# The border between two blocks: residual before split, squares behind the parts, softmax sums behind the gated output

## The reference, cut to what matters

```
x  = x + rms_norm(mixer(rms_norm(x, pre_norm_w)), post_norm_w)      # first block
h  = rms_norm(x, norm_g)                                            # second block
qa, kca, vca, ksa, vsa, kwa, vwa, za, ga, qb, kb, vb, zb = split(h @ w_in_2)
o_a = g0 * compressed(qa) + g1 * selected(qa) + g2 * windowed(qa)   # g = sigmoid(ga)
o_b = banded(qb, kb, vb)                                            # with sinks
x  = x + concat(o_a * silu(za), o_b * silu(zb)) @ w_out_2
out = rms_norm(x, final_g)
```

## Time and profile before

| | |
|---|---|
| median of 3 runs (lowest to highest) | 1212.39 us (1212.36 to 1212.54) |
| the profiled execution's own time | 1211.66 us |
| its span in the trace | 1209.8 us |
| PE busy | 1196.0 us, 99% |
| DVE busy | 750.3 us, 62% |
| ACT busy | 608.6 us, 50% |
| POOL busy | 98.7 us, 8% |

### The profile page before, as it was taken

The page is one execution under the profiler, slowest core; times in us unless marked ns, Lnnn a source line. Parts: engine busy times, 40 slices in busy tenths (PEclk is TensorE's granted clock), DMA queues, the critical chain, the costliest instruction groups (busy, mean ns, idle before and its releaser), DMA issues.

```text
span 1209.8 us, 16240 instructions
## 1 busy us (share of the span) xinstructions
PE 1196.0 (99%) x6422; PEld 999.4 (83%) x6422; DVE 750.3 (62%) x1002; ACT 608.6 (50%) x896; POOL 98.7 (8%) x134
## 2 busy tenths in 40 slices
PE   9999999999999999999999999999999999999997
PEld 8888888888878888888888888888777778788886
DVE  5778876765666656555554455576665665676654
ACT  6665655544324555444444444464446547566443
POOL 0000011189200000000000000010000000000000
PEclk9999999999999999999999999999999999999999
DMA  8666664576544545665666686656747555454862
GB/s 286 172 204 177 187 195 141 163 211 193 175 142 122 174 124 145 217 193 176 200 184 195 194 286 200 201 177 200 239 154 239 164 173 186 121 164 144 297 197 95
DMA packets 143259, 224.03 MB, mean 185 GB/s; under 512 B 12176, under 2 KB 63056, under 8 KB 142160
## 3 DMA queue, kind: packets, MB, share of 16 engines
q1 hardware_dynamic: 140800, 212.50, 57.4%
q0 software_dynamic: 2064, 9.45, 2.2%
q10 hardware_dynamic: 320, 1.06, 0.2%
HBM read 218.25 MB, written 4.72 MB: 184 GB/s over the span
## 4 chain that ended last, share of the span: by engine, by line
PE 94%; DVE 3%; ACT 1%; issue 1%; DMA 0%; POOLq 0%; SPq 0%; POOL 0%; ACTq 0%; DVEq 0%
PE acc L2030 64%; PE acc L2009 10%; PE acc L2011 5%; PE aux L1900 4%; PE acc L1960 2%; PE acc L2021 2%; PE aux L2245 1%; PE aux L2273 1%; DVE lo_w L1357 1%; PE aux L1983 1%; PE aux L2135 1%; PE aux L2238 1%; PE aux L2266 1%; ACT hi_w L981 0%; DVE cv L1476 0%
## 5 line engine op out<-in xcount | busy, mean ns | idle before, releaser
L1357 DVE TENSOR_TENSOR lo_w<-raw_w,hi_w 128x1024 fp32r<-128x1024 f32 (+1 forms) x381 | 464.6, 1226 | 340.0 <-ACT hi_w L981 338.6
L981 ACT ACTIVATE hi_w<-raw_w 128x1024 fp32r<-128x1024 f32 (+1 forms) x381 | 395.3, 1053 | 268.7 <-PE acc L2030 188.5
L2030 PE MATMUL acc<-hi_w,h_both 128*128 128x512 f32 (+1 forms) x1632 | 521.6, 392 | 0.3 <-DVE h_both L1721 0.3
L2030 PEld LDWEIGHTS acc<-hi_w,h_both 128*128 128x128 f32 x1632 | 304.6, 188 | 66.9 <-issue 4.9
L2030 PE MATMUL acc<-lo_w,h_both 128*128 128x512 f32 (+1 forms) x816 | 315.0, 386 | 0.0
L2009 PE MATMUL acc<-h_both,hi_w 128*128 128x512 f32 x576 | 204.1, 399 | 0.5 <-DVE lo_w L1357 0.5
L2030 PEld LDWEIGHTS acc<-lo_w,h_both 128*128 128x128 f32 x816 | 153.5, 188 | 28.1
L2011 PE MATMUL acc<-h_both,lo_w 128*128 128x256 f32 x576 | 160.9, 279 | 0.0
L2009 PEld LDWEIGHTS acc<-h_both,hi_w 128*128 128x128 f32 x576 | 108.2, 188 | 26.3 <-DVE lo_w L1357 0.9
L2011 PEld LDWEIGHTS acc<-h_both,lo_w 128*128 128x128 f32 x576 | 108.6, 189 | 0.1
L2030 PE MATMUL acc<-hi_w,m_hi 128*128 128x512 f32 x224 | 87.7, 391 | 0.0
(11 more groups left out here) (361 smaller groups left out, 1196.9 us busy)
## 6 DMA issues: line engine op xcount, KB each, us to landing
raw_w<-in_w_in SPq DMA_DIRECT2D x279, 512.0 KB, 3.9
raw_w<-in_w_out SPq DMA_DIRECT2D x64, 512.0 KB, 4.6
raw_w<-in_w_branch_a SPq DMA_DIRECT2D x16, 512.0 KB, 4.7
raw_w<-in_w_branch_b SPq DMA_DIRECT2D x16, 512.0 KB, 4.8
raw_w<-in_cmp_k_w SPq DMA_DIRECT2D x8, 512.0 KB, 6.3
raw_w<-in_cmp_v_w SPq DMA_DIRECT2D x8, 512.0 KB, 7.1
x_in<-in_x SPq DMA_DIRECT2D x8, 256.0 KB, 7.3
x<-in_x POOLq DMA_DIRECT2D x1, 2048.0 KB, 10.8
```

The lines of the kernel that those rows point to most:

```text
L981: act.activation(piece_flat(hi_w[slot], no), piece_flat(raw_w[no % RAW_SLOTS], no), ACT.Copy).then_inc(*hi_ready.event(no))
L1357: dve.tensor_tensor(piece_flat(lo_w[slot], no), piece_flat(raw_w[no % RAW_SLOTS], no), piece_flat(hi_w[slot], no).bitcast(F32), ALU.subtra ...
L2030: i = pe.matmul(to[:, t, 0:group.cols], x[at], w[:, k], start=first and k == 0 and m == 0, stop=last and k == n - 1 and m == 2)
```

## The change

Three groups of edits, all in the order of steps. Nothing is computed otherwise.

- Tick c: on DVE and ACT the tick's split of piece c+4 stands behind `h2_hi(1, 0)`, `h2_lo(1, 0)` and `residual(0, 1)`, no longer ahead of `y_last(1)`.
- Ticks c+3 to c+9: `residual(3, t)` goes from c+3 to c+4, behind the parts of quarter 2; the splits of pieces c+7 and c+8 are placed by hand, the latter behind the parts of quarter 3; the eight squares go from c+3, c+5 and c+6 to c+6 and c+7, all behind the parts of quarter 3; `norm2` and `rope_tables` come a tick later.
- Compressed attention: DVE's sums, clamp, inverse and gate go from tick 347 to tick 348, that is behind both `flip("y", 2, t)` and the split of piece 350. The key by which a tick's steps are sorted also names `catt(2)`.

```diff
-    if tick >= TICKS or tick not in FULL or tick == FINAL - 2 or -3 <= tick - BORDER <= 4:
+    if tick >= TICKS or tick not in FULL or tick == FINAL - 2 or -3 <= tick - BORDER <= 6:
...
         for n in ahead:
-            at(c + tick, "split", c + n)
             if n == 4:
                 at(c, "y_last", 1)
+                at(c, "h2_hi", 1, 0)
+                at(c, "h2_lo", 1, 0)
+                at(c, "residual", 0, 1)
+            at(c + tick, "split", c + n)
...
-    at(c, "h2_hi", 1, 0)
-    at(c, "h2_lo", 1, 0)
-    at(c, "residual", 0, 1)
...
     for t in range(NT):
-        at(c + 3, "residual", 3, t)
         at(c + 3, "h2_flip", 2, t)
     at(c + 3, "split", c + 5)
-    at(c + 3, "sq2", 0)
     for t in range(NT):
         at(c + 4, "h2_hi", 2, t)
         at(c + 4, "h2_lo", 2, t)
+    for t in range(NT):
+        at(c + 4, "residual", 3, t)
     at(c + 4, "split", c + 6)
-    at(c + 5, "sq2", 1)
+    at(c + 5, "split", c + 7)
     for t in range(NT):
         at(c + 5, "h2_flip", 3, t)
         at(c + 6, "h2_hi", 3, t)
         at(c + 6, "h2_lo", 3, t)
-    at(c + 6, "sq2", 2)
-    at(c + 6, "sq2", 3)
-    at(c + 7, "norm2")
-    at(c + 8, "rope_tables")
+    at(c + 6, "split", c + 8)
+    for n in range(4):
+        at(c + 6 + n // 2, "sq2", n)
+    at(c + 8, "norm2")
+    at(c + 9, "rope_tables")
...
-        tick.sort(key=lambda step: (step[0], step[-1]) not in (("att", 1), ("att", 2)))
+        tick.sort(key=lambda step: (step[0], step[-1]) not in (("att", 1), ("att", 2), ("catt", 2)))
...
                     dve.tensor_tensor(both, both, over_heads(cmask[:, 1].rearrange("p t c -> p (t c)"), HEADS),
                                       ALU.mult).then_inc(*dve_did.event("cprob"))
+                if n == 3:
                     dve.wait_ge(*dve_did.after("cprob"))
                     link(dve.tensor_reduce(cden, s, AXX, ALU.add))
```

## The result

The changed kernel takes 1214.2 us (median of 15 runs, 1213.6 to 1215.6), the kernel before 1212.1 us beside it (15 runs, 1211.57 to 1212.67): ratio 1.0018, interval 1.0012 to 1.0025. The rise is 2.1 us where 1.7 was forecast. The profiled execution took 1214.52 us, its span is 1212.7 us.

What follows compares the result with a forecast made beforehand. PE, busy 1196.0 of 1209.8 us, was taken as the bound. Terms -0.57 - 0.43 + 3.33 - 0.62 = +1.71 us gave 1213.4 us profiled and a median of 1214.1 us; range 1211.4 to 1215.3 us.

Steps and rivals of the forecast that it cites:

- Part 1: Tick c: with the residual ahead of the split, PE's transposes of quarter 0, tile 1, start earlier: -0.57 us.
- Part 2: Quarter 2's low parts come 0.9 us earlier, so PE's wait at piece c+5 goes wholly: -0.43 us.
- Part 3: Squares and norm behind quarter 3's parts lengthen the chain to the rotated keys; PE waits 3.33 us.
- Part 4: Compressed attention: the 0.98 us wait for the copy goes, a bank wait before the scores comes: net -0.62 us.
- (a): Border: ACT and DVE finish the norm in PE's shadow, so gains without the cost: 1210.8 us; chance 0.10.
- (b): Border: only c+10's split is late; a shorter root chain adds nothing at the keys' transposes: 1212.0 us; chance 0.10.
- the port conflict: Norm's root on POOL: a DVE split with two SBUF inputs blocks its first operation; without blocking 0.7 us less.
- (c): Late piece c+4 keeps the first stall, losing 0.57; bank wait may eat the other 0.62: 1214.7 to 1215.3 us; chance 0.16.

Runs made afterwards that it cites:

- the second of the later profiles: The changed kernel, nothing altered, profiled once more as the second of three extra executions: 1213.64 us.
- the kernel with the old ticks: Changed kernel with the eight squares, the norm's sum and the tables back in their old ticks: 1211.0 us against 1211.89 for the kernel before, ratio 0.9992.

## Why the prediction was right, point by point

**Part 1.** Forecast -0.57, measured -0.59 in the changed kernel and alone. The residual starts 0.59 earlier, counted from the transposes before it (788.68 - 786.06 = 2.62 us, against 788.18 - 784.97 = 3.21). The 0.23 that was to stay as lost shows no idle in brackets, where about 0.1 was forecast, but 3.42 us for a stretch that could take 3.21 is that loss.

**Part 2.** Forecast -0.43, measured -0.55, which is beyond the bound of 0.43 on record. The wait took more than its gap: the first product behind it is followed only after 0.31 us (799.52 to 799.83), where 0.23 is usual, and the rest of the piece loses another 0.04. The low parts start 1.30 us behind the transposes of quarter 2 (forecast 1.29), and the split of c+5, the loads and the 2 MB store cost nothing that a wait shows.

**Part 3.** Forecast +3.33, measured +3.31; the chain was summed to 19.37 us and is 19.35. Its split into two places was right as well: 1.16 for the 1.2 at piece c+10 and 2.14 for the 2.1 before the keys. What made the sum safe was that nearly every term came from rows of the same instructions in start-to-start times; in the trace after, none is off by more than 0.07 us. The one that was worked out from another shape, 0.95 for the split of c+8, is 0.95 in the trace.

**Part 4.** Forecast -0.62, measured -0.63 at the scores: 0.98 won at the products and the rest given back at the banks, as shown by the 0.1 us between the addition's end and the scores. The forecast stopped there, and that was too early. DVE's queue runs on without idle up to the multiplication for the transposes of `z`, which in the kernel before ended at 1063.95 us, 0.15 before PE began them. Counted from the keys, PE would now come 0.55 us earlier and DVE is only 0.39 earlier, so PE waits again, and the part is worth -0.39 (-0.41 in the kernel with the sums alone). The term was 0.23 us too large.

**The sum.** By marks, up to the transposes of `z`, the change costs -0.59 - 0.55 + 3.31 - 0.39 = +1.78 us, for the +1.71 on record; the first mark to these transposes is 280.91 us after and 279.13 before, and 280.93 in the second of the later profiles. That the sum is so close is in part luck: part 2 was forecast 0.12 too small and part 4 0.23 too large. The medians give +2.1. The 0.3 us between are not in the stretch of the change, nor behind it: from the transposes of `z` to the end all thirteen profiles of this document take 145.69 to 145.78 us. They lie in the opening, or in half-clock executions. Four long executions out of 15 explain 0.1 (the median of the other eleven is 1214.07). The opening differs from execution to execution by more than the rest: the first mark is at 785.18, 785.67 and 786.06 in three executions of the changed kernel, and at 785.23 to 786.03 in the nine profiles of the other kernels, while the one profile of the kernel before has 784.97, the earliest of all. For the eight kernels of the experiments, too, marks and medians agree within 0.3 us.

**The rivals.** (a) needed the norm in PE's shadow: the kernel with the old ticks does that. (b) needed a shorter root: taking the port conflict away shortens it by 0.71 us, and the split that it has to pass eats that. (c) needed a late piece c+4: no kernel with the split behind the residual waits there. Its second half, a wait that eats the gain of part 4, came to 0.24 of the 0.62, behind the scores.

## What to carry to other kernels

Work that nobody waits for yet may still be cheap only where it stands: before moving it behind something urgent, sum the chain that it heads, in start-to-start times, and compare that with the time in which the bounding engine covers the same stretch. The better place is not later but in the idle time that the timeline shows in brackets (here 1.1 to 2.3 us before a block of parts in the changed kernel, and 0.70 us before each low part in the kernel before). And when single gains of half a microsecond drown in the runs, the distance between two marks of the bounding engine, on each side of the edit, still shows them. The second mark belongs behind the last instruction that the moved work delays: here 0.24 of 0.63 us came back as a wait 6 us behind the mark that looked like the end.

## What the hardware showed that had not been expected

A standstill of TensorE can cost more than its length, and not in each execution. Behind waits of 1.00 and 1.99 us, with 4.9 us of matmuls between them, one of three profiles of the changed kernel shows the granted clock at half (1.2 GHz) for over 3 us; the two others have 1.00 (2.4 GHz) there. With a single wait of 4.02 us it was at half for over 6 us. Two waits may not be needed: with late squares alone there is only the one of 1.97 us behind the transposes of quarter 3, and three of ten executions were long at a mean clock of 0.997, though neither profile of that kernel shows a fall in that stretch. The price depends on what comes next: 1.56 us where dense matmuls followed, and 0.6 us of six at half clock where the next wait would have taken the rest of the time. The kernel with the split of c+11 behind the tables broke the same standstill into 1.00, 0.69 and 1.25 us; none of its ten runs was over 1214.57 us. That smaller pieces are the reason was not tested.
